# Hybrid attention and convolution block: first two k tiles of the latent projection by token halves, and three pieces of work moved

## The reference

```python
def modulate(h, shift, scale):
    return h * (1 + scale[:, None, :]) + shift[:, None, :]
...
    sh1, sc1, g1, sh2, sc2, g2 = jnp.split(mod_lat, 6, axis=-1)      # mod_lat = silu(c) @ w_ada + b_ada
    csh1, csc1, cg1, csh2, csc2, cg2 = jnp.split(mod_ctx, 6, axis=-1)
    h = modulate(rmsnorm(x, norm1_g), sh1, sc1)                      # x: 512 tokens x 1024
    hc = modulate(rmsnorm(ctx, norm1_g), csh1, csc1)                 # ctx: 256 tokens
    p = h @ w_in                                                     # kv latent 256 | rope key 32 | q latent 384 | conv x, B, C | gates
    pc = hc @ w_in[:, :KR_END]
    kn_c, kr_c, v_c = mla_kv(pc, kv_norm_g, w_ukv, None)
    kn_l, kr_l, v_l = mla_kv(p, kv_norm_g, w_ukv, ang)
    qn, qr = mla_query(p, q_norm_g, w_uq, ang)
    o = mla_latent(qn, qr, concat(kn_c, kn_l), concat(kr_c, kr_l), concat(v_c, v_l))    # 8 heads, 768 keys
    # gated_merge: y_conv = (b_gate * dwconv(c_gate * x_in, conv_w, conv_b)) @ w_conv_out
    x = x + g1[:, None, :] * gated_merge(p, o, conv_w, conv_b, w_attn_out, w_conv_out, w_o)
    x = x + g2[:, None, :] * conv_ffn(modulate(rmsnorm(x, norm2_g), sh2, sc2), w_up, ffn_conv_w, ffn_conv_b, w_down)
    # then a final rmsnorm of x
```

## Time and profile before

| | |
|---|---|
| median of three runs | 841.5 us (839.99 to 844.02) |
| the profiled execution | 841.12 us, of which the span is 839.1 us |
| granted TensorE clock, mean | 0.989 |
| TensorE busy | 811.4 us (97%), 3937 matmuls |
| VectorE, ScalarE, GpSimd busy | 467.1, 373.6, 381.2 us |
| longest chain by engine | PE 89%, DVE 5%, ACT 3% |
| HBM read | 95.17 MB, mean 116 GB/s |

### The profile page before, as it was taken

One profiled execution on the slowest core, in us unless ns is written; L12 is line 12 of the kernel. 1 busy time (PEld: TensorE's weight loads), 2 busy tenths in 40 slices (PEclk: granted clock), 3 DMA queues, 4 the chain that ended last, 5 costly groups with the idle time before them and its releaser, 6 DMA issues.

```text
span 839.1 us, 11438 instructions
## 1 busy us (share of the span) xinstructions
PE 811.4 (97%) x3937; PEld 676.4 (81%) x3937; DVE 467.1 (56%) x635; ACT 373.6 (45%) x592; POOL 381.2 (45%) x197
## 2 busy tenths in 40 slices
PE   4799999999999999999999999999999999999996
PEld 4578977888888888888788988888888888888884
DVE  4787596788888467877303565555555555000005
ACT  6566456666667322322423664334444433221125
POOL 2623494436442554555544054444444444443434
PEclk9899999999999999999899999999999999999998
DMA  8661242111110688777273033333333332322212
GB/s 288 208 193 48 54 113 64 33 44 52 26 51 27 212 261 267 237 231 221 78 249 101 1 101 116 87 97 100 100 100 100 91 93 92 100 101 100 85 42 101
DMA packets 120289, 97.82 MB, mean 117 GB/s; under 512 B 13660, under 2 KB 106105, under 8 KB 120249
## 3 DMA queue, kind: packets, MB, share of 16 engines
q1 hardware_dynamic: 120137, 97.26, 37.9%
q10 hardware_dynamic: 112, 0.04, 0.0%
HBM read 95.17 MB, written 2.10 MB: 116 GB/s over the span
## 4 chain that ended last, share of the span: by engine, by line
PE 89%; DVE 5%; ACT 3%; POOL 1%; issue 1%; DMA 1%; SPq 0%; POOLq 0%; DVEq 0%; ACTq 0%
PE ps L422 25%; PE ps L424 24%; PE ps L423 24%; PE ps L1725 7%; PE ps L1832 3%; PE ps L1821 2%; DVE wlo L341 1%; PE ps L1585 1%; DMA adaraw<-w_ada_dram 1%; POOL wlo L341 1%; ACT work L749 1%; PE ps L1899 0%; PE ps L1917 0%; DVE x L1520 0%; ACT work L1073 0%
## 5 line engine op out<-in xcount | busy, mean ns | idle before, releaser
L341 POOL TENSOR_TENSOR wlo<-raw,whi 128x1024 fp32r<-128x1024 f32 (+4 forms) x125 | 281.2, 2257 | 363.7 <-ACT whi L333 363.2
L422 PE MATMUL ps<-hhi,whi 128*128 128x512 f32 (+1 forms) x520 | 196.2, 377 | 0.2 <-DVE hlo L1467 0.2
L424 PE MATMUL ps<-hhi,wlo 128*128 128x512 f32 (+1 forms) x520 | 195.8, 377 | 0.0
L423 PE MATMUL ps<-hlo,whi 128*128 128x512 f32 (+1 forms) x520 | 195.7, 376 | 0.0
L333 ACT ACTIVATE whi<-raw 128x1024 fp32r<-128x1024 f32 (+4 forms) x125 | 118.2, 957 | 132.4 <-PE ps L424 77.5
L424 PEld LDWEIGHTS ps<-hhi,wlo 128*128 128x128 f32 x520 | 97.9, 188 | 18.1
L422 PEld LDWEIGHTS ps<-hhi,whi 128*128 128x128 f32 x520 | 97.9, 188 | 18.1 <-DVE hlo L1467 0.4
L423 PEld LDWEIGHTS ps<-hlo,whi 128*128 128x128 f32 x520 | 97.9, 188 | 17.8
L1495 DVE SCALAR_TENSOR_TENSOR work<-ps,prm,work 128x511 f32<-128x511 f32 x44 | 33.0, 750 | 75.0 <-ACT work L1049 74.0
L1400 DVE SCALAR_TENSOR_TENSOR adacc<-ada,cvec,adacc 128x1024 f32<-128x1024 f32 x28 | 60.7, 2204 | 18.5 <-DMA ada<-w_ada_dram 18.4
L422 PE MATMUL ps<-whi,fhi 128*128 128x512 f32 x176 | 69.8, 396 | 0.0
(11 more groups left out here) (290 smaller groups left out, 1533.2 us busy)
## 6 DMA issues: line engine op xcount, KB each, us to landing
raw<-w_up_dram SPq DMA_DIRECT2D x88, 256.0 KB, 3.2
ada<-w_ada_dram SPq DMA_DIRECT2D x32, 512.0 KB, 6.3
raw<-w_in_dram SPq DMA_DIRECT2D x56, 256.0 KB, 4.3
raw<-w_down_dram SPq DMA_DIRECT2D x44, 256.0 KB, 2.7
adaraw<-w_ada_dram SPq DMA_DIRECT2D x32, 256.0 KB, 4.8
raw<-w_o_dram SPq DMA_DIRECT2D x16, 256.0 KB, 3.1
xt<-x_dram SPq DMA_DIRECT2D x4, 512.0 KB, 7.3
raw<-w_attn_out_dram SPq DMA_DIRECT2D x8, 256.0 KB, 2.8
```

Source lines behind the costliest of these rows:

```text
L341: ins = (engine or nc.gpsimd).tensor_tensor(out=l, in0=r, in1=h.bitcast(F32), op=ALU.subtract)
L422: pe.matmul(o, l[0], r[0], start=start, stop=False)
L423: pe.matmul(o, l[0], r[1], start=False, stop=False)
L424: return pe.matmul(o, l[1], r[0], start=False, stop=stop)
```

## The change

- *Latents by token halves.* `latents` takes a half (256 tokens). The order on TensorE becomes: token blocks 0 and 1, `first_sums(0)`, token block 2, `first_sums(1)`, k tile 0 of the first half, `spread_rinv(2)`, token block 3, k tile 1 of the first half, `spread_rinv(3)`, k tile 0 of the second half, then k tile 1 of the second half around the four `mod_sums`. ScalarE and VectorE get `stream_half_hi` and `stream_half` for the four quarters. PSUM banks of transposes and spreads are dealt out anew: token block 3 goes to the banks of block 2 (5 and 7), and `spread_rinv(2)` and `(3)` go to bank 3, which the first sums use.
- *Loads.* The weights of k tiles 0 and 1 are loaded ahead of token blocks 2 and 3.
- *Context pieces.* ScalarE scales pieces 4 to 7 in one go behind `rinv_copy(1)`; GpSimd adds them ahead of `latent_lo(1)`.
- *Second convolution unit.* `U_CC0` is split behind head 2 and not head 3, on ScalarE and GpSimd.
- *First taps.* `conv_mid(0)` moves from value tile 4 to 1 on ScalarE, `conv_taps(0)` from behind the second maximum to behind `value_lo(1)` on VectorE.

```diff
-LOWER_BANK, UPPER_BANK = (4, 6, 0, 4, 5, 5), (5, 1, 7, 5, 7, 7)
+LOWER_BANK, UPPER_BANK = (0, 1, 5, 5, 5, 5), (4, 6, 7, 7, 7, 7)
+RINV_BANK = (2, 2, 3, 3)
...
 # SyncE, the loads
-            for t in range(TT):
-                ada_load(t - SLOTS)
-                token_load(t)
+            ada_load(0 - SLOTS)
+            token_load(0)
+            ada_load(1 - SLOTS)
+            token_load(1)
+            latent_load(0)
+            ada_load(2 - SLOTS)
+            ada_load(3 - SLOTS)
+            latent_load(1)
+            token_load(2)
+            token_load(3)
...
 # GpSimd
             latent_lo(0)
-            latent_lo(1)
             for k in range(4, DT):
                 first_context_add(k)
-            for k in range(2, DT):
+            for k in range(1, DT):
                 latent_lo(k)
...
-                if h in (1, 3, 4, 5):
-                    u = {1: U_UQ[3], 3: U_CC0, 4: U_V, 5: U_N}[h]
+                if h in (1, 2, 4, 5):
+                    u = {1: U_UQ[3], 2: U_CC0, 4: U_V, 5: U_N}[h]
                     split_lo(pool, u, u % SLOTS)
...
 # ScalarE
+            def stream_half_hi(k, half):
+
+                act.wait_ge(s("mods1"), 2 * k + 2)
+                act.wait_ge(s("xT_low"), 2 * half + 2)
+                to = slice(*HALVES[half])
+                nc.scalar.activation(hhi[:, k, to], xnT[:, k, to], ACT.Identity, bias=shift[:, 0, k:k + 1],
+                                     scale=gain[:, 0, k:k + 1]).then_inc(s("h_hi"), 1)
...
             rinv_copy(1)
+            latent_hi(0)
+            context_scale(4)
+            context_scale(5)
+            context_scale(6)
+            context_scale(7)
+            stream_half_hi(0, 0)
             token_rms(2)
+            latent_hi(1)
             rinv_copy(2)
             token_rms(3)
-            latent_hi(0)
+            stream_half_hi(1, 0)
             rinv_copy(3)
-            context_scale(4)
-            context_scale(5)
-            stream_hi(0)
-            stream_hi(1)
-            context_scale(6)
-            context_scale(7)
-            latent_hi(1)
+            ada_hi(0)
+            stream_half_hi(0, 1)
+            stream_half_hi(1, 1)
...
-                if h in (1, 3, 4, 5):
-                    u = {1: U_UQ[3], 3: U_CC0, 4: U_V, 5: U_N}[h]
+                if h in (1, 2, 4, 5):
+                    u = {1: U_UQ[3], 2: U_CC0, 4: U_V, 5: U_N}[h]
                     split_hi(act, u, u % SLOTS)
...
-                if kt == 4:
+                if kt == 1:
                     act.wait_ge(s("q_rope"), 3 * HEADS)
                     conv_mid(0)
...
 # VectorE
+            def stream_half(k, half):
+
+                part = 2 * half + k
+                lo, hi = HALVES[half]
+                dve.wait_ge(s("mods1"), 2 * k + 2)
+                dve.wait_ge(s("xT_low"), 2 * half + 2)
+                nc.vector.tensor_scalar(ht[:, k, 0:T // 2], xnT[:, k, lo:hi], gain[:, 0, k:k + 1], shift[:, 0, k:k + 1],
+                                        ALU.mult, ALU.add).then_inc(s("h_t"), 1)
+                dve.wait_ge(s("h_t"), part + 1)
+                dve.wait_ge(s("h_hi"), part + 1)
+                nc.vector.tensor_tensor(out=hlo[:, k, lo:hi], in0=ht[:, k, 0:T // 2], in1=hhi[:, k, lo:hi].bitcast(F32),
                                         op=ALU.subtract).then_inc(s("h_lo"), 1)
...
+            token_rinv(0)
             first_token(2)
             first_token(3)
-            token_rinv(0)
             scale_low(0)
-            scale_up(0)
             token_rinv(1)
             first_token(4)
             first_token(5)
             scale_low(1)
-            token_rinv(2)
             first_token(6)
             first_token(7)
+            dve.wait_ge(s("gain0"), 1)
+            first_mods(0)
+            stream_half(0, 0)
+            scale_up(0)
+            scale_up(1)
+            token_rinv(2)
+            first_mods(1)
+            stream_half(1, 0)
             scale_low(2)
+            scale_up(2)
             token_rinv(3)
-            scale_up(1)
             scale_low(3)
-            dve.wait_ge(s("gain0"), 1)
-            for k in range(2):
-                first_mods(k)
-                stream_value(k)
-                stream_lo(k)
-            scale_up(2)
+            stream_half(0, 1)
+            stream_half(1, 1)
             scale_up(3)
...
             for kt in range(KT):
                 value_lo(kt)
+                if kt == 1:
+                    conv_taps(0)
...
             maxima(1)
-            conv_taps(0)
             normalize(0)
...
 # TensorE
                 if t == 3:
-                    pe.wait_ge(s("xT_low"), 1)
-                    pe.wait_ge(s("xT_up"), 1)
+                    pe.wait_ge(s("xT_low"), 3)
+                    pe.wait_ge(s("xT_up"), 3)
...
                 wait(pe, s("rinv_row"), t)
-                pe.matmul(ps[:, 2, t * P:(t + 1) * P], small[:, 24 + t:25 + t].to_broadcast([P, P]), ident[:],
+                if t == 2:
+                    pe.wait_ge(s("mods1"), 4)
+                pe.matmul(ps[:, RINV_BANK[t], t * P:(t + 1) * P], small[:, 24 + t:25 + t].to_broadcast([P, P]), ident[:],
...
-            for t in range(TT):
+            every = range(QT + KVT)
+            for t in range(2):
                 token_columns(t)
                 spread_rinv(t)
+            first_sums(0)
+            token_columns(2)
+            first_sums(1)
+            latents(0, every, 0)
+            spread_rinv(2)
+            token_columns(3)
+            latents(1, every, 0)
+            spread_rinv(3)
+            latents(0, every, 1)
             pe.wait_ge(s("sel"), 1)
-            first_sums(0)
-            first_sums(1)
-            pe.wait_ge(s("xT_up"), 2)
             pe.wait_ge(s("rinv_row"), TT)
-            every = range(QT + KVT)
             for c_ in range(CHUNKS):
-                latents(2 * c_, every)
-                if c_ == 0:
-                    latents(1, (0, 1))
+                if c_:
+                    latents(2 * c_, every)
+                else:
+                    latents(1, (0,), 1)
...
```

More of the change, by code:

```diff
@@ L502, in _ @@
             for c_ in range(CHUNKS):
-                latent_load(2 * c_)
-                latent_load(2 * c_ + 1)
+                if c_:
+                    latent_load(2 * c_)
+                    latent_load(2 * c_ + 1)
                 if c_ in (1, 2):
@@ L757, in rinv_copy @@
                 act.wait_ge(s("rinv_ps"), t + 1)
[L758 removed]
+                nc.scalar.activation(rinv_rows[:, t * P:(t + 1) * P], ps[:, RINV_BANK[t], t * P:(t + 1) * P], ACT.Copy).then_inc(s("rinv_row"), 1)
             def ada_hi(u):
@@ L800, in _ @@
             rinv_copy(1)
+            latent_hi(0)
[4 more added lines that the diff above has]
+            stream_half_hi(0, 0)
             token_rms(2)
+            latent_hi(1)
             rinv_copy(2)
             token_rms(3)
-            latent_hi(0)
+            stream_half_hi(1, 0)
             rinv_copy(3)
-            context_scale(4)
-            context_scale(5)
-            stream_hi(0)
-            stream_hi(1)
-            context_scale(6)
-            context_scale(7)
-            latent_hi(1)
+            ada_hi(0)
+            stream_half_hi(0, 1)
+            stream_half_hi(1, 1)
             for c_ in range(1, CHUNKS):
                 for u in range(4 * c_ - 4, 4 * c_):
-                    ada_hi(u)
+                    if u > 0:
+                        ada_hi(u)
                 mod_rows1(c_)
@@ L1608, in late_columns @@
                 pe.wait_ge(s("prm_loaded"), 16 * 9)
-                pe.wait_ge(s("xT_up"), 3)
+                pe.wait_ge(s("xT_up"), TT)
                 pe.wait_ge(s("first_ctx"), DT - 1)
@@ L1626, in mod_columns, with latents @@
                 last.then_inc(s("cols1_ps"), 1)
-            def latents(k, tiles):
+            def latents(k, tiles, half=None):
                 pe.wait_ge(s("win_lo"), k + 1)
-                pe.wait_ge(s("h_lo"), k + 1)
+                pe.wait_ge(s("h_lo"), k + 3 if half is None else 2 * half + k + 1)
+                at = slice(0, T) if half is None else slice(*HALVES[half])
                 for m in tiles:
+                    if (k, half) == (0, 0):
+                        if m == 2:
+                            pe.wait_ge(s("rinv_row"), 2)
+                        if m >= QT:
+                            pe.wait_ge(s("xT_up"), m - QT + 1)
                     w = (tuple(t[:, k % 3, m * P:(m + 1) * P] for t in (lqhi, lqlo)) if m < QT else
                          tuple(t[:, k, (m - QT) * P:(m - QT + 1) * P] for t in (lkhi, lklo)))
-                    last = mm3(pe, ps[:, LATENT_BANK[m], :], w, (hhi[:, k, :], hlo[:, k, :]), k == 0, k == DT - 1)
+                    last = mm3(pe, ps[:, LATENT_BANK[m], at], w, (hhi[:, k, at], hlo[:, k, at]), k == 0 and half == 0, k == DT - 1)
                     if k == DT - 1:
                         last.then_inc(s("lat_ps"), 1)
-                    elif m == QT + KVT - 1:
```

(7 more changed lines are left out.)

7 lines of the change are left out of this document (4 added, 3 removed).

## The result

The changed kernel takes **848.51 us** (median of 6 runs, 847.38 to 850.71), the kernel before beside it 842.86 us (6 runs, 839.99 to 844.02). Ratio 1.008, 95% interval 1.0065 to 1.0095: **slower by 0.8%**. The two medians themselves lie 5.65 us apart; by the interval the change costs 5.5 to 8.0 us. The profiled execution took 847.6 us with a span of 845.6, against 839.1 before.

The account below looks back on a forecast made before the run. TensorE, busy for 97% of the span, was taken to bound the kernel. The start's +6.9 us and the two later edits' +0.3 gave +7.2 on the profiled 841.12 us: 848.3 us, range 843.0 to 851.0 (8 in 10).

Parts of the forecast that it names:

- late edits: Second convolution unit and first taps, between the start and the scores: together +0.3 us.
- Head start: Start, up to k tile 0's first half: first latents at 20.5 us, about 3.4 us sooner.
- First stall: Ahead of token block 3's transposes: TensorE waits 4.1 us for ScalarE's and VectorE's steps behind `spread_rinv(2)`.
- Second stall: Ahead of k tile 0's second half: TensorE waits 2.3 us for ScalarE's steps and VectorE's low part.
- `ada_lo`: VectorE's low parts of `w_ada`: four from 38.5 us take 4.9 us, not 8.6, giving back 3.7 us.
- Fourth `mod_sums`: End of the start: 44.3 us against 37.4 before, with VectorE's chain last, so +6.9 us.
- The unit's part: Second convolution unit: its 2.1 us wait goes, `values(0)` then waits for `ck_lo`, 1.0 us of gain remains.
- The taps: `conv_mid(0)` ahead of the first keys' copy on ScalarE: `keys(0, 1)` waits, 1.3 us taken back.
- The stall is shorter: Rival, start: same order but the clock is up early, start costs 3.9 us, total 844.0 us; 16%.
- The second stall alone is there: Rival, start: as if the first wait were half hidden, `mod_sums` end at 41, total 843.7 us; 5%.
- The query gain stays: Rival, queries: start +6.9 us but queries -2.2 us, total 845.8 us; 15%.
- The head start wins: Rival, block 3's transposes: everything runs 3.4 us ahead with uncontended `ada_lo`, queries add -2.2, total 835.5 us; 7%.

Follow-up runs that it names:

- x7: Changed kernel with GpSimd's additions of context pieces 4 to 7 held back until the first high part of `w_ada`; 851.03 us, ratio 1.0106 to the kernel before.
- x5: Changed kernel with `spread_rinv(2)` inside the half-tile, `spread_rinv(3)` right behind token block 3, block 2's scalings ahead of the waiting low part; 840.28 us, ratio 0.9984 to before.
- x4: Kernel before with the second convolution unit split behind head 2 and the first taps moved among the values, start unchanged; 841.48 us, ratio 1.0001.
- x2: Kernel before with only the second convolution unit split behind head 2 instead of head 3; 839.84 us, ratio 0.9978.
- x6: Kernel before with only its context pieces scaled and added early, whole k tiles kept; 839.82 us, ratio 0.9968.
- x8: Kernel before with early context pieces, first reciprocal and first modulation brought forward, part of `latents(1)` moved behind the `mod_sums`; 837.69 us, ratio 0.9948.

## Why the prediction was right, and which terms were off

The forecast was +7.2 us, as 6.9 from the start and 0.3 from the late edits. Measured: 7.4 at the fourth `mod_sums`, 7.85 at `transposes(0)`, 6.5 in the span, and 0.8% in the ratio. That 848.3 and the median of 848.51 agree to 0.2 us is in part luck: the kernel before had 842.86 in these runs, not 841.5, and the terms below missed in both directions. The mechanism, two stalls of TensorE made by the order on ScalarE and VectorE, was right. Point by point:

- **Head start: 3.4 us forecast, 2.1 measured.** Mis-sized. Of the 1.3 us, 0.3 is TensorE's own row, which ended at 20.8 (`first_sums(0)`, taken at 0.50 us, took 1.01). The other 1.0 is its wait for the first quarter, whose value and low part took 1.20 and 1.51 us, where I had at most 0.5 us of delay in sum. x7 shows the two at 0.41 and 0.43 without GpSimd's additions beside them. I had read the lock from `ada_lo` (2.2 us against 1.2) and supposed that it could cost only that half again. The Trainium skill (SBUF — State Buffer, section "SBUF: two separate sides") has a VectorE operation with two SBUF inputs, or in a mode that uses two ports, and a GpSimd one keep each other out for a whole instruction. By that a short instruction can wait out a long one: one of the changed kernel's additions took 5.54 / 4 = 1.4 us, and 0.43 + 1.4 is 1.8. The trace agrees so far that the low part took 1.51. The value has one SBUF tensor and two columns as input, and took 1.20 too; whether it ran in such a mode no run here shows.
- **First stall: 4.1 us forecast, 4.04 measured.** By the steps named: spread, copy, square and root, high part, low part, two scalings. It began and ended 1 us later, for the smaller head start. x5 takes it away and with it, and the second, 8.1 us.
- **Second stall: 2.3 forecast, 2.48 measured**, ended by the low part.
- **`ada_lo`: from 38.5 and 4.9 us for four forecast; 38.52 and 4.62 measured.** The start agrees partly by luck: the clock rose at 34.1, in the last matmuls of k tile 1's first half, which the steps had at half speed to the end. That rise can be read from the matmuls alone (0.21 us apart up to 34.1, 0.12 behind it); the granted clock reads 1.00 from 22 to 34 us. Block 3 began 1.1 us late; the transposes held TensorE 0.3 us less than their 1.92, and the faster clock gave back another 0.5.
- **Fourth `mod_sums`: 44.3 forecast, 44.8 measured.** Here the path was wrong by a little, though the number came out. I took VectorE's chain to be last, but its fourth low part ended at 38.52 + 4.62 = 43.14, which by the same 0.95 gives 44.1. TensorE was last: it stood at nothing between 37.37 and 44.82. My own terms said so too: `mod_sums(0)` reached at 40.8, and 16 matmuls of 0.23 us behind it, make 44.5, and I had left out the 16. Half speed for the second half of k tile 0 was right only because the clock, up at 34.1, had fallen to 0.50 again from 38 to 41 behind the stall (last section). At full speed its 18 matmuls ahead of `mod_sums(0)` would have taken some 1.6 us less, and VectorE's chain would have been last.
- **Late edits: +0.3 forecast, -0.3 measured on the kernel before.** The unit's part was right in mechanism and size (1.0 of 2.1 forecast, 0.8 measured, the wait for `ck_lo` 0.61). The taps were mis-sized: 1.3 us taken back, against 0.5. I counted on a keys copy later by the whole `conv_mid`, but it moved 0.6 us (keys at 131.07 in x4, 130.44 in x2), and a part is lost again by `transposes(0)`. In the changed kernel the same stretch is 100.63 us, 0.6 longer than before, so there the +0.3 looks better than it was: a half-clock stretch at 106 to 109 lies in it, which costs 1.7 us and hides the wait of 0.6 for `ck_lo`. Without it I estimate 99.5, near x4's 99.74.
- **The rivals.** "The stall is shorter" and "The second stall alone is there" fall with 4.04 us. "The query gain stays" needed -2.2 us from the late edits, and falls with x4's -0.3. "The head start wins" is what x5 approaches when both lists are reordered, and even then it wins 0.16%, 1.3 us, and not 6, since the low parts beside GpSimd and a wait of 1.28 us ahead of k tile 2 stay.

## What to carry to other kernels

When a tile is halved so that work can start sooner, write down what the other engines have in their lists between the two halves: a step that the second half needs and that is queued behind the first half's low part turns the head start into a stall. Here that order cost 8.1 us. With it mended the halves brought no gain that whole tiles did not: x5, with halves and early context pieces, has 0.9984, x6, with early context pieces alone, 0.9968, and x8, whole tiles in a better order, 0.9948. Before you move GpSimd's work, look at which of VectorE's operations it will then stand beside: x7 freed the first quarter, slowed the third and fourth, and lost 0.26% against the changed kernel. And try each idea of a bundle by itself: the two that helped (context pieces early with the order put right, and the unit) gave 0.66% together, while the bundle lost 0.8%.
